# Dense feed-forward layer: four passes of 256 rows replaced by one pass over all rows with Strassen block products

## The reference, cut to what matters

```
def _rmsnorm(x, gain):
    xf = x.astype(F32)
    y = xf * lax.rsqrt(jnp.mean(xf * xf, axis=-1, keepdims=True) + EPS)
    return (y * gain.astype(F32)).astype(x.dtype)

def _swiglu(h, w_gate, w_up, w_down):
    return (jax.nn.silu(h @ w_gate) * (h @ w_up)) @ w_down
...
        x = x + jnp.concatenate([a, r], axis=-1) @ w_out[l]
        h = _rmsnorm(x, ffn_norm[l])
        if l % 2 == 0:
            j = l // 2
            x = x + _swiglu(h, dense_w_gate[j], dense_w_up[j], dense_w_down[j])
```

## Time and profile before

| what | value |
|---|---|
| time, median of 3 runs | 5563.79 us (5557.76 to 5565.94) |
| time of the profiled execution | 5557.37 us |
| its span | 5554.7 us |
| busy: TensorE, VectorE, ScalarE, GpSimd | 93%, 49%, 40%, 6% |
| mean granted clock of TensorE | 0.96 of full |
| dense layer, first to last product | 1833.7 to 2582.0 us |

### The profile page before, as it was taken

One profiled execution on the slowest core, in us unless ns is written; L12 is line 12 of the kernel. 1 busy time (PEld: TensorE's weight loads), 2 busy tenths in 40 slices (PEclk: granted clock), 3 DMA queues, 4 the chain that ended last, 5 costly groups with the idle time before them and its releaser, 6 DMA issues. The chain is left out here.

```text
span 5554.7 us, 97507 instructions
## 1 busy us (share of the span) xinstructions
PE 5144.0 (93%) x38308; PEld 4510.9 (81%) x38309; DVE 2744.3 (49%) x4394; ACT 2225.6 (40%) x3437; POOL 344.9 (6%) x564
## 2 busy tenths in 40 slices
PE   7996989889999899997989988999999999999994
PEld 5675967677777899997877777999999999999994
DVE  2597545332844555554147434444444555555544
ACT  2454236333443444444234433333334444444432
POOL 0111100000600000000014001000000000000001
PEclk8997999999999999998999998999999999999997
DMA  2110010321002655553100434444444554555444
GB/s 86 38 65 18 0 37 1 113 69 34 0 20 109 244 210 195 199 213 127 48 21 18 130 126 165 159 164 159 164 159 176 193 195 180 202 198 188 181 159 190
DMA packets 104541, 687.39 MB, mean 124 GB/s; under 512 B 12320, under 2 KB 16304, under 8 KB 63280
## 3 DMA queue, kind: packets, MB, share of 16 engines
q1 hardware_dynamic: 90752, 639.74, 31.5%
q0 software_dynamic: 8816, 27.44, 1.3%
q10 hardware_dynamic: 4800, 17.83, 0.8%
HBM read 622.67 MB, written 62.29 MB: 123 GB/s over the span
## 5 line engine op out<-in xcount | busy, mean ns | idle before, releaser
L3393 DVE TENSOR_TENSOR experts_low<-experts_raw,experts_high 128x1024 fp32r<-128x1024 f32 x678 | 810.4, 1223 | 954.1 <-ACT experts_high L3320 954.0
L3236 PE MATMUL ps<-experts_xs_high,experts_high 128*128 128x256 f32 (+1 forms) x3584 | 1030.8, 288 | 21.5 <-issue 10.9
L3236 PE MATMUL ps<-experts_xs_low,experts_high 128*128 128x256 f32 (+1 forms) x3584 | 1028.9, 287 | 0.0
L3236 PE MATMUL ps<-experts_xs_high,experts_low 128*128 128x256 f32 (+1 forms) x3584 | 1028.8, 287 | 0.0
L3320 ACT ACTIVATE experts_high<-experts_raw 128x1024 fp32r<-128x1024 f32 x678 | 687.8, 1049 | 36.6 <-DMA experts_raw<-experts 36.6
L3236 PEld LDWEIGHTS ps<-experts_xs_high,experts_high 128*128 128x128 f32 x3584 | 673.3, 188 | 33.7 <-issue 25.2
L3236 PEld LDWEIGHTS ps<-experts_xs_low,experts_high 128*128 128x128 f32 x3584 | 673.8, 188 | 8.3
L3236 PEld LDWEIGHTS ps<-experts_xs_high,experts_low 128*128 128x128 f32 x3584 | 673.5, 188 | 0.0
L2913 PE MATMUL ps<-dense_xs_parts,dense_high 128*128 128x256 f32 x2816 | 499.6, 280 | 7.1 <-DVE dense_low L3022 5.9
L2913 PEld LDWEIGHTS ps<-dense_xs_parts,dense_high 128*128 128x128 f32 x2816 | 437.0, 189 | 14.3 <-issue 7.9
L3228 PE MATMUL ps<-experts_high,experts_hid_high 128*128 128x512 f32 x1120 | 438.5, 391 | 0.0
(11 more groups left out here) (538 smaller groups left out, 9094.3 us busy)
## 6 DMA issues: line engine op xcount, KB each, us to landing
experts_raw<-experts SPq DMA_DIRECT2D x226, 1536.0 KB, 6.2
dense_raw<-dense SPq DMA_DIRECT2D x90, 1536.0 KB, 6.9
mixT<-w_in SPq DMA_DIRECT2D x36, 512.0 KB, 3.7
y_slot<-mla_blank SPq DMA_DIRECT2D x15, 1152.0 KB, 21.6
out_proj_raw<-w_out SPq DMA_DIRECT2D x48, 256.0 KB, 2.7
proj_keys_raw<-w_in SPq DMA_DIRECT2D x20, 512.0 KB, 3.7
x_mixed<-mixT SPq DMA_DIRECT2D x16, 512.0 KB, 2.6
h_rows<-out_proj_rows SPq DMA_DIRECT2D x16, 512.0 KB, 2.6
```

The lines of the kernel that those rows point to most:

```text
L3236: last = nc.tensor.matmul(ps[:, m, 0:width], w[:, u, m, c], x[:, k, 0:width], start=(k == 0 and i == 0), stop=(k == KD - 1 and i == 2))
L3393: nc.vector.tensor_tensor(low[:, v, t, :], raw[:, v % NR, t, :], high[:, v, t, :].bitcast(F32), ALU.subtract).then_inc(split, 1)
```

## The change

`swiglu_passes` is gone and `dense_products` takes its place, called from inside the first mixing layer. It works in two parts.

**Part 1, gate and up, all 1024 rows.** Columns of the hidden layer are taken in 11 pairs `p` of two blocks of 128 (`c` = 0, 1), the contraction in two halves of 512 (`k`), and the rows in two halves of 512. That is a 2 by 2 by 2 block product, made with 7 block products in place of 8, for gate (`m` = 0) and up (`m` = 1): 14 operands `o` per pair, 154 in all. Each operand is one 128x512 sum or difference of weight blocks (`sum_operand`, on VectorE), rounded by ScalarE, split by VectorE, and then used in 12 products of 128x128 by 128x512. The 7 right-hand operands are differences of quarters of the rows (`t1` made by VectorE, three made by GpSimd with 128x2048 subtractions), turned by TensorE in 14 `turn`s of 8 transposes, and kept on chip for all pairs (`x_parts`). Results are combined in PSUM by going on summing on a bank, after ScalarE has copied out the value that another result needs (`copied`), and by VectorE additions onto these copies (`added`). silu(gate) * up, 4 quarters of 128x512 per pair, is written to DRAM (`hidden`) by GpSimd's queue.

**Part 2, down.** For each half `t` of the rows, 22 steps `f` load the down weights (512 KB) and a 128x512 piece of `hidden` (256 KB), split both, and make 24 products of 128x128 by 128x512, summed in all eight PSUM banks. VectorE adds the residual (`evict`), and GpSimd's queue writes the rows.

In `product_and_norm` with `keep=True` the normalized rows stay on chip in `mixT`, and the writes to `h_rows` fall away; x itself gets a tile of its own (`x_rows`).

In the diff, the first block of `dense_products` with waits is SyncE's (`room`), then come GpSimd's, TensorE's and VectorE's.

```
-def product_and_norm(core, name, xT, weights, source, gain_row, normed, out=None, router=False):
+def product_and_norm(core, name, xT, weights, source, gain_row, normed, out=None, router=False, keep=False):
...
-    x = as_rows(xT)
+    x = st.sb("x_rows", [P, NT, D]) if keep else as_rows(xT)
...
+                if keep:
+                    continue
                 sp.wait_ge(scaled, b + 1)
                 sp.dma_start(normed[b * P:(b + 1) * P, :], row(b)).then_inc(stored[b % 2], 16)
...
-def swiglu_passes(core, name, NC, weights, out, experts=None, tiles=None, residual=None):
...
+def dense_products(core, name, rows, weights, hidden, residual, out):
...
+    NF = DFF // P
+    PAIRS = NF // 2
+    A11, S1, S2, A12, S3, S4, A22 = range(7)
+    NA = 14 * PAIRS
+    SETS = 4
...
+    q11, q21 = rows[:, 0:4, 0:HALF], rows[:, 0:4, HALF:D]
+    q12, q22 = rows[:, 4:8, 0:HALF], rows[:, 4:8, HALF:D]
+    t1 = kept[:, :, :]
+    turn_source = (q11, t1, q11, q21, q12, q22, q11)
...
+            def room(n):
+                before = n - 8
+                if before < 0:
+                    if n >= 4:
+                        sp.wait_ge(turned, 12)
+                elif before < 4 * PAIRS:
+                    p, j = divmod(before, 4)
+                    sp.wait_ge(split, 14 * p + 2 * (S4 if j < 2 else A22) + j % 2 + 1)
+                else:
+                    sp.wait_ge(split, NA + before - 4 * PAIRS + 1)
...
+            pool.wait_ge(t1_made, 1)
+            pool.wait_ge(turned, 2)
+            nc.gpsimd.tensor_tensor(q11, q22, t1, ALU.subtract).then_inc(t_made, 1)
+            nc.gpsimd.tensor_tensor(q12, q22, q12, ALU.subtract).then_inc(t_made, 1)
+            pool.wait_ge(t_made, 1)
+            pool.wait_ge(turned, 6)
+            nc.gpsimd.tensor_tensor(q11, q21, q11, ALU.subtract).then_inc(t_made, 1)
+            for p in range(PAIRS):
+                for k, (c, t) in enumerate(hid_parts):
+                    pool.wait_ge(hid_made, 4 * p + k + 1)
+                    pool.dma_start(hidden[2 * p + c][:, t * HALF:(t + 1) * HALF], hid_places[k]).then_inc(stored[k], 16)
...
+            def turn(h):
+                q, half = divmod(h, 2)
+                if q == 1:
+                    pe.wait_ge(t1_made, 1)
+                if q in (2, 4, 6):
+                    pe.wait_ge(t_made, q // 2)
+                if h >= 8:
+                    pe.wait_ge(x_low, 7 if h == 8 else h)
+                elif h >= 2:
+                    pe.wait_ge(x_low, h - 1)
...
+            def multiply(o):
+                p, q, m = o // 14, o % 14 // 2, o % 2
+                pe.wait_ge(split, o + 1)
+                if p == 0:
+                    pe.wait_ge(x_low, 2 * q + 2)
...
+                for k in range(4):
+                    c = slice(k * P, (k + 1) * P)
+                    for i, (w, x) in enumerate(((0, 0), (0, 1), (1, 0))):
+                        last = nc.tensor.matmul(bank(p, q, m), w_parts[:, o % 4, w, c], x_parts[:, q, x, k, :],
+                                                start=opens and k == 0 and i == 0, stop=k == 3 and i == 2,
+                                                skip_group_check=not opens)
+                last.then_inc(product, 1)
+
+            for h in range(4):
+                turn(h)
+            for o in range(NA):
+                multiply(o)
+                if o + 4 < 14:
+                    turn(o + 4)
...
+            nc.vector.tensor_tensor(t1, q12, q11, ALU.subtract).then_inc(t1_made, 1)
+            place(0)
+            place(1)
+            split_operand(0)
+            place(2)
+            split_operand(1)
+            place(3)
+            sum_operand(2)
+            sum_operand(3)
+            split_operand(2)
+            split_operand(3)
+            for o in range(NA):
+                p, q, m = o // 14, o % 14 // 2, o % 2
+                if o + 4 < NA:
+                    sum_operand(o + 4)
+                dve.wait_ge(product, o + 1)
...
+                if o + 4 < NA:
+                    split_operand(o + 4)
                 else:
...
+                    split_down(o + 4 - NA)
+                if o + 4 < 14:
+                    place(o + 4)
```

More of the change, by code:

```diff
@@ L1713, in _ @@
                 sp.wait_ge(written, 16 * NT)
-            for i in range(2):
+            for i in range(0 if keep else 2):
                 sp.wait_ge(stored[i], 16 * NT // 2)
@@ L2726, in route @@
     st.end()
-def swiglu_passes(core, name, NC, weights, out, experts=None, tiles=None, residual=None):
-    nc, d = core.nc, core.dram
+def dense_products(core, name, rows, weights, hidden, residual, out):
+    nc = core.nc
     st = Stage(core, name)
[L2744 to L2781, removed]
-    def passes(eng, body, otherwise=None):
-        if not routed:
-            with eng.Fori(0, n_pass // 2, 1) as i:
-                for v in range(2):
-                    body(2 * i + v, SLOTS, v * NC % NB)
-            return
-        with eng.Fori(0, n_pass, 1) as j:
-            n = eng.value_load(tiles[0:1, bass.ds(j, 1)], min_val=0, max_val=2)
-            with eng.If(n > 1):
-                body(j, SLOTS, 0)
-            with eng.If(n == 1):
-                body(j, P, 0)
-            if otherwise is not None:
-                with eng.If(n == 0):
-                    otherwise(j)
@@ new lines, in dense_products @@
+    NF = DFF // P
[3 more added lines that the diff above has]
+    SETS = 4
+    raw = st.sb("raw", [P, 4, D])
+    sums = st.sb("sums", [P, 2, HALF])
+    kept = st.sb("kept", [P, 4, HALF])
+    w_parts = st.sb("w_parts", [P, 4, 2, HALF], F32R)
+    x_parts = st.sb("x_parts", [P, 7, 2, 4, HALF], F32R)
+    loaded = [st.sem(f"loaded{i}") for i in range(8)]
+    stored = [st.sem(f"stored{i}") for i in range(4)]
+    (t1_made, t_made, turned, x_high, x_low, summed, rounded, split, product, copied, added, silu_done, hid_made,
+     down, finished, y_in, evicted, written) = (
+        st.sem(n) for n in ("t1_made", "t_made", "turned", "x_high", "x_low", "summed", "rounded", "split", "product", "copied",
+                            "added", "silu", "hid_made", "down", "finished", "y_in", "evicted", "written"))
@@ L2873, in _ @@
+            pool.wait_ge(written, 128)
         @block.tensor
         def _(pe):
[L2875 to L2939 removed]
@@ L2998, in _, with place, round_operand @@
-            passes(act, one_pass, lambda j: write(j))
-            act.wait_ge(written, 16 * (n_pass + 1))
+            def place(h):
+                q, half = divmod(h, 2)
+                act.wait_ge(turned, h + 1)
+                nc.scalar.activation(x_parts[:, q, 0, 2 * half:2 * half + 2, :], turn_banks(h), ACT.Copy).then_inc(x_high, 1)
+            def round_operand(o):
+                p, q, m = o // 14, o % 14 // 2, o % 2
+                if q in (S1, S2, S3, S4):
+                    act.wait_ge(summed, sums_made(p, q, m))
+                else:
+                    n = 4 * p + (2 if q == A22 else 0) + m
+                    act.wait_ge(loaded[n % 8], arrivals(n))
+                if o >= 4:
+                    act.wait_ge(product, o - 3)
+                nc.scalar.activation(w_parts[:, o % 4, 0, :], operand(p, q, m), ACT.Copy).then_inc(rounded, 1)
@@ L3001, in _ @@
+            for s in range(SETS, 2 * NF):
+                round_down(s)
         @block.vector
         def _(dve):
[L3004 to L3016 removed]
@@ L3071, in swiglu_passes @@
+            for s in range(SETS, 2 * NF):
+                if s == NF + SETS - 1:
+                    evict(0)
+                split_down(s)
+            evict(1)
     st.end()
```

454 lines of the change are left out of this document (218 added, 236 removed).

## The result

The changed kernel takes 5484.37 us (median of 4 runs, 5478.05 to 5489.44), the kernel before 5564.86 us beside it (4 runs): ratio 0.9857, 95% interval 0.9845 to 0.9869. The forecast was 5484 us. The profiled execution took 5489.44 us.

The account below looks back on a forecast made before the run. TensorE's columns bound the dense layer. Entry 1825.3 + cold start 2.9 + products 660.7 + turns 8 + stalls 6 + end 7.5 = 2510.4 against 2589.8, 79.4 us less: 5484 us on the median, range 5472 to 5502.

Parts of the forecast that it names:

- Products: Dense layer, both parts: 2904 products of 512 columns at 227.5 ns each on TensorE, 660.7 us (658.3 to 663.0).
- Fixed part of a product: Any TensorE product: 5.9 ns paid whatever its width, solved from 116.7 ns for 256 columns and 227.5 for 512.
- the rival on weight loads: TensorE products: fewer weight loads save more than 5.9 ns each, at most 277 us more, 5207 us; chance 0.01.
- Entry: Dense layer's start: first product 9.8 us after the stage's start, at 1825.3, the first split waiting behind GpSimd's subtraction.
- First pair: First column pair of part 1, with turns between products: expected to last 55 us.
- Cold start: First products of the dense layer: 5.9 us at clock 0.50 as before, 2.9 us of lost work.
- stalls: First pair: TensorE waits for placements and behind GpSimd's subtractions, 6 us (0 to 14.4).
- the port costs nothing: Rival at the entry and first pair: GpSimd's subtractions fall where VectorE waits anyway, 5 us less, 5479; chance 0.12.
- Ten pairs and part 2 uncharged: Part 1 after the first pair, and part 2: other engines and loads stay hidden behind TensorE, nothing charged.
- The rival on handoffs: Operands and steps of both parts: a wait at each gives back 59 us, 5543 (half: 5514); chance 0.15.
- the rival on part 2's loads: Part 2: loads bind, a step lasts 10.5 us in place of 5.5, 220 us, 5705; chance 0.03.
- The end: Last product to the next stage's first DMA: 7.5 us, against 7.85 before.

Follow-up runs that it names:

- the quarters: GpSimd's three 128x2048 entry subtractions cut into four 128x512 pieces each, against the changed kernel: 5478.81 us, stage 690.2 us, 4.4 less.
- the second profiles: The kernel before and the changed kernel each run once more without any change: 5564.23 us and 5482.31 us.

## Why the prediction was right, and where it was off

- **Products** (660.7 us): right in kind, 0.8 ns too dear. It took 227.5 ns between two cadences; 226.7 held in part 1 and 239.8/1056 = 227.1 in part 2, 658.7 us in all. All waits included, first product to end of last took 675.2 against 677.6.
- **Fixed part of a product** (5.9 ns, in the rival on weight loads): too small. With 512 against 256 columns on the same tiles it is 13.3 ns. It was solved from a narrow product with 10.0 ns besides its columns and a wide one with more, as if both had the same. The sum didn't use it, since it took wide products from rows of wide products. No 107 ns came back for a weight load, and the rival of 5207 us is out: a product of 256 columns with its load takes 120.0 ns, of which 106.7 go with the columns.
- **Entry** (9.8 us to the first product): 8.9. The mechanism was right and is shown by the quarters. The first two turns took 3.6 us and not 4.1 (granted clock 0.53), GpSimd's first subtraction 4.53 us and not 4.8, and the split ended 0.55 us behind it.
- **First pair** (55 us): 54.1, from 1829.93 to 1873.16 + 48 x 0.2267. Cold start and stalls together were 8.9 in the sum and 54.1 - 38.1 - 7.9 = 8.1 in the trace. The wait foreseen at turn 6 (the seventh), behind the third subtraction (3 us), is there with 3.69. Starts part the two terms: the low clock costs 2.9 us (2.9 in the sum) and stalls some 5.1 (6). But the 2.9 came otherwise than foreseen, 1.4 in the first product and 1.5 behind the wait at the seventh turn; a cold start in one stretch of 5.9 us, as before, there was none. That the sizes agree is luck.
- **The rival "the port costs nothing"**: out by 3.00, 3.92 and 4.37 us for 0.69. Its price, 5 us, was near: the quarters gave back 4.4, though they leave some of the stretching.
- **Ten pairs and part 2 uncharged**: right; no wait over 0.3 us, and one third fewer products took nearly one third less there (265.2 us for 391.8). The rival on handoffs is out; the rival on part 2's loads too, at 5.45 us a step (239.8/44).
- **The end** (7.5 us): wrong. The step said that "only two additions are left behind the last product (1.3 us), but GpSimd's queue issues", and took 7.5 us without working them out; it had the queue's issue in view, not what the engine does after the landing. Of the 10.5 us the drain is 4.5; through SyncE 5.0 are left. 3.0 us too little, against 1.0 too much at the entry and 2.4 too much from the first product to the last: 0.4 us in sum, and so partly luck.
- **Median and profile**: 80.5 us between the medians, 79.8 between the pieces of the table. The two profiled spans differ by only 66.9, since the code ahead of the layer was later and the code behind it longer in this execution, and that was scatter, as the second profiles show.

## What to carry to other kernels

Count TensorE's columns first and price a product by start-to-start intervals at its own width; when nothing else waits, the difference is the answer. A mean over a stretch hides joints, so look at single starts. Then look at the joints, where the engines meet: a long GpSimd instruction on SBUF stretches VectorE's of two SBUF tiles to its own end. Cut in pieces it does less harm (4.4 us of the stage here), though each piece still stretches what lies beside it; and let a stage's last writes go through SyncE, so that GpSimd's drain falls early. A wait of TensorE costs more than its length where the clock is low behind it. Compare such mends by the stage's length, not by whole runs.

## What the runs showed of the hardware that was not expected

- GpSimd's `DRAIN` at the end of the dense layer takes 4471 ns, to the nanosecond, in all eight profiles in which GpSimd issues the last writes, right after the last has landed. It takes 9.9 to 13.3 us in the five in which it comes early in the stage and transfers of others still run. At the 32 barriers of line L117 of the same execution it takes 34 to 51 ns. What it does in that time no run tells.
- A product of fp32r operands with its own weight load costs 13.3 ns beside one clock a column (120.0 and 226.7 ns), in either order of the halves; in the kernel before the narrow ones took 116.7.
- VectorE and GpSimd stretch each other: beside each other, twelve pieces of GpSimd's subtractions took 19.6 us in place of 14.1 for the same work in three instructions, while VectorE's instructions of two SBUF tiles took up to 1.77 us in place of 0.69.
- After a wait of 3.69 us TensorE's granted clock was 0.50 and a turn took 1.62 us in place of 0.79; after one of 2.5 us with a third of the products left out, products were 427 ns apart in place of 226.7.
